# Weight loads of a two-layer mixer and mixture-of-experts kernel: halves, earlier slots, gathers among products

## The chip, the cores and the metric

One core of one Trainium2 chip. The metric is the device time of one launch in microseconds (us); lower is better. Times inside an execution are counted from the start of its span.

## The reference

Two layers on 256 tokens of width 1024, all float32. Layer 0 has a mixer of mLSTM and RG-LRU, layer 1 one of S5 and gated linear attention (GLA). Each is followed by a layer norm over `ALPHA * h + mixer(h)`, then a mixture of experts, then a second norm:

```python
scores = sigmoid(x @ router_w)            # 64 experts, 8 groups
... 8 experts per token, from the 4 best groups
h = silu(x @ w_gate[e]) * (x @ w_up[e])   # [tokens of e, 256]
y = (h @ w_down[e]) * weight              # summed over the 8 experts
out = y + (silu(x @ sw_gate) * (x @ sw_up)) @ sw_down
```

The gate, up and down weights of an expert are 1 MB each, so the experts of a layer are 64 x 3 MB.

## The kernel before

The stages run one after another: `mix0`, `moe0`, `mix1`, `moe1`. Each engine has its program written out by hand, with semaphores between them; SP issues nearly all transfers, in program order, on one DMA queue.

**Where weights go.** The dense weights (mixer, shared expert) pass through `weight_ring`, two halves of 2 MB: `ring_load` (L273) waits until the reader of the load two before is done (`ring_free`, L260), then issues. The experts' weights go to four slots of `expert_weights`, three parts each: gate, up, down (`expert_load` L305, `first_load` L375). The mixers use the same memory for their own data, so slots can be filled only when that data is dead.

**The experts on PE.** `pe_moe` starts with the shared expert's gate and up products (`shared_up`, L995 to L1039, products at L999), for which it waits for the ring half `sh_gu`; the router's products and DVE's choice of experts run between. Then experts go in pairs, 32 a layer. Pairs with even numbers use slots 0 and 1, odd ones slots 2 and 3. For each pair `octets` (L1103) does:
- the gate and up products over eight chunks `c` (L1124, two experts side by side), after waits for the weights, and then counts `gu_full`;
- the scatter of the pair before (L1050), a turn of the gates, the turn of the hidden values (L1138), and two gathers of token rows for the octet after (`gather`, L1075 to L1082); in the last pairs products of the shared expert's down weights and `ALPHA * h` instead (L1086, L1067);
- the down products (L1168), in two halves of 512 columns, each with its own count (`y_lo_full`, `y_hi_full`).

Before the first pair all eight gathers of the first octet are done (L1180 to L1185), each into one of three banks, and ACT (even `c`) and DVE (odd `c`) copy them out.

**The refills.** In `sp_moe` (L383) the first fill of the slots comes in this order: router weights and bias, ring half `sh_gu`, slots 0 and 1 (layer 0, after the stores of `mix0`) or 0 to 2 (layer 1, after PE's product `o1`), ring half `sh_d`, and after `h_ready` the other slots and the norm's parameters. `group` (L404) then refills: for a pair of slots it waits for `gu_full` of the pair that used them, issues two gates and two ups, waits for `y_hi_full`, issues two downs.

**The mixers where the change touches them.** `sp_mix0` and `sp_mix1` load the ring, store and fetch two S5 tables (`s5_b`, `s5_c`) that `mix0`'s DVE program computes for `mix1`: `dve_s5_inputs` (L1696, twelve operations in two halves) stands before the tiles `cols`, `bc0`, `bc1`, whose banks PE uses next. In `mix1` PE starts with products from the fetched `s5_c` (`pe_direct`, L659, products at L667) as soon as DVE has written a first part of the norm (L1472).

Of the kernel before, what the change touches and what calls it, by code (L numbers as in the profile page):

```python
# [86 lines left out]
def build(nc, A, out, stages=("mix0", "moe0", "mix1", "moe1")):  # L87
    ctx = ExitStack()
    with ctx:
# [112 lines left out]
        for l in range(2):  # L202
            MO[l]["gu_in"] = [sem(f"moe{l}_gu_in{s}") for s in range(NSLOT)]
            MO[l]["d_in"] = [sem(f"moe{l}_d_in{s}") for s in range(NSLOT)]
# [100 lines left out]
        def expert_load(sp, m, l, e, s):  # L305
            src_g = A["exp_w_gate"][l, e].rearrange("(p c) f -> p (c f)", c=KC)
            src_u = A["exp_w_up"][l, e].rearrange("(p c) f -> p (c f)", c=KC)
            sp.dma_start(ew[:, s, 0:EW], src_g).then_inc(m["gu_in"][s], 16)  # L308
            sp.dma_start(ew[:, s, EW:2 * EW], src_u).then_inc(m["gu_in"][s], 16)  # L309
# [47 lines left out]
        def sp_mix1(sp, npass):  # L357
# [13 lines left out]
            for name in ("qk1", "v1", "r1", "glu1", "out_a1", "out_b1"):  # L371
                ring_load(sp, ring_no[name])
            sp_ln_params(sp, k, A["ln1_w"][1], A["ln1_b"][1])

        def first_load(sp, m, l, s):  # L375
            expert_load(sp, m, l, s, s)
            sp.dma_start(ew[:, s, 2 * EW:3 * EW], down_src(l, s)).then_inc(m["d_in"][s], 16)

        EARLY_SLOTS = (2, 3)
# [3 lines left out]
        def sp_moe(sp, l):  # L383
# [5 lines left out]
            ring_load(sp, ring_no[f"sh_gu{l}"])  # L389
            early = EARLY_SLOTS[l] if k else 0  # L390
            if l == 0:
                sp.wait_ge(M1["stored"], 32)
            else:
                sp.wait_ge(*B1.full("o1"))
            for s in range(early):
                first_load(sp, m, l, s)
            ring_load(sp, ring_no[f"sh_d{l}"])
            if k:
                sp.wait_ge(S["h_ready"], TT * k)
            for s in range(early, NSLOT):  # L400
                first_load(sp, m, l, s)
            sp_ln_params(sp, k, A["ln2_w"][l], A["ln2_b"][l])

            def group(base, it):  # L404

                for u in range(2):

                    sp.wait_ge(m["gu_full"], (base - 1) * 2 + u + 1)
                    for s in (2 * u, 2 * u + 1):
                        expert_load(sp, m, l, it * NSLOT + s, s)  # L410
                    sp.wait_ge(m["y_hi_full"], (base - 1) * 2 + u + 1)
                    for s in (2 * u, 2 * u + 1):
                        sp.dma_start(ew[:, s, 2 * EW:3 * EW], down_src(l, it * NSLOT + s)).then_inc(m["d_in"][s], 16)

            with sp.Fori(1, NE // NSLOT) as it:
                group(it, it)
            sp.wait_ge(m["npass"], 1)
            npass = sp.value_load(npass_i[0:1, 0:1], min_val=1, max_val=MAX_PASS)
            with sp.If(npass > 1):
                with sp.Fori(1, npass) as ps:  # L420
                    with sp.Fori(0, NE // NSLOT) as it:
                        group(ps * (NE // NSLOT) + it, it)
# [679 lines left out]

# [1014 lines left out]
```

## Time and profile before

| | |
|---|---|
| median of 3 runs | 1257.88 us (1257.76 to 1260.94) |
| the profiled execution | 1257.82 us |
| its span | 1256.1 us |
| PE busy | 1166.2 us (93%) |
| DVE, ACT, POOL busy | 489.3, 193.3, 47.3 us |
| read from HBM | 456.51 MB, 368 GB/s over the span |
| granted clock of TensorE, mean | 0.995 |

The span is what the profiler saw; the time of an execution is 1.7 us more. PE is TensorE's matmul, SPq the queue of SyncE that issues transfers. A row of the timeline has start, duration, engine, line and operation, and in brackets the idle time before it and what ended it. L numbers are lines of the kernel. A product in float32 is shown as two records.

### The profile page before, as it was taken

Reading aid. Unit: us, or ns where it says so; the run is one execution under the profiler, and the core shown is the slowest. Engines: PE = TensorE matmul, PEld = TensorE weight load, DVE = VectorE, ACT = ScalarE, POOL = GpSimd, SP = SyncE. Lnnn points to the kernel's source line nnn. Section 1 sums busy time; section 2 is a strip of 40 time slices with the busy share of each in tenths; the row PEclk is TensorE's granted clock in tenths of the full one; section 3 lists DMA queues with packets and bytes.
Section 4 is the critical chain, followed back from the end, with each engine's and each line's share of the span. In section 5 each row is a group of like instructions: output and inputs, shape, how many; then the busy total and the mean of one; then the engine's idle time right before and its main releaser. Section 6 shows DMA issues by size and latency. Waiting matters only on the chain.

```text
span 1256.1 us, 17816 instructions
## 1 busy us (share of the span) xinstructions
PE 1166.2 (93%) x7245; PEld 567.4 (45%) x7245; DVE 489.3 (39%) x1059; ACT 193.3 (15%) x330; POOL 47.3 (4%) x78
## 2 busy tenths in 40 slices
PE   9999999988888888999899999999888988889996
PEld 8774833333333333333387657333333333333332
DVE  5994733332323233332327256332333233232224
ACT  3231311111111111110122312111111111111102
POOL 6200100000000000000000001000000000000000
PEclk9999999999999999999999999999999999999999
DMA  9775989999999999999953278999999999999993
GB/s 347 205 301 193 421 344 422 420 421 421 421 421 422 422 422 422 422 421 421 399 176 134 96 288 340 419 420 422 420 421 422 420 422 422 422 422 421 421 422 154
DMA packets 76125, 463.78 MB, mean 369 GB/s; under 512 B 8544, under 2 KB 9888, under 8 KB 25376
## 3 DMA queue, kind: packets, MB, share of 16 engines
q1 hardware_dynamic: 75920, 462.37, 90.5%
q8 instruction: 47, 0.77, 0.2%
q10 hardware_dynamic: 144, 0.52, 0.1%
q14 instruction: 14, 0.11, 0.0%
HBM read 456.51 MB, written 6.36 MB: 368 GB/s over the span
## 4 chain that ended last, share of the span: by engine, by line
PE 51%; DMA 42%; SPq 3%; DVE 2%; issue 1%; ACT 1%; DVEq 0%; POOL 0%; POOLq 0%
DMA expert_weights<-in_exp_w_up 40%; PE bank L1124 23%; PE bank L1168 5%; PE bank L652 4%; PE bank L638 3%; PE bank L999 2%; PE bank L726 2%; PE bank L742 2%; SPq L308 2%; PE bank L1050 1%; PE bank L753 1%; DMA expert_weights<-s_rows 1%; PE bank L1079 1%; SPq L309 1%; DMA s_rows<-hidden 1%
## 5 line engine op out<-in xcount | busy, mean ns | idle before, releaser
L1124 PE MATMUL bank<-expert_weights,weight_ring 128*64 128x512 f32 x1024 | 226.8, 595 | 30.9 <-DMA expert_weights<-in_exp_w_up 30.9
L1168 PE MATMUL bank<-expert_weights,hiddenT 128*32 128x512 f32 x2048 | 233.0, 595 | 10.0 <-ACT weight_ring L1379 5.0
L1989 DVE TENSOR_TENSOR hidden<-silu_gate,bank 128x256 f32<-128x256 f32 x64 | 27.0, 422 | 424.3 <-ACT silu_gate L1388 424.3
L1124 PEld LDWEIGHTS bank<-expert_weights,weight_ring 128*64 128x64 f32 x1024 | 81.1, 137 | 175.5 <-issue 175.2
L1124 PE MATMUL bank<-expert_weights,hT 128*64 128x512 f32 x512 | 118.4, 603 | 30.7 <-DMA expert_weights<-in_exp_w_up 30.4
L1168 PEld LDWEIGHTS bank<-expert_weights,hiddenT 128*32 128x32 f32 x2048 | 60.0, 109 | 146.0 <-issue 119.4
L1124 PE MATMUL bank<-expert_weights,octet_high 128*64 128x512 f32 x512 | 116.0, 592 | 0.0
L1388 ACT ACTIVATE silu_gate<-bank 128x256 f32<-128x256 f32 x64 | 24.6, 385 | 471.1 <-PE bank L1124 471.1
L2001 DVE TENSOR_SCALAR y_top<-bank,slot_gate 128x512 fp32r<-128x512 f32 x64 | 48.1, 751 | 108.1 <-PE bank L1168 108.1
L1124 PEld LDWEIGHTS bank<-expert_weights,hT 128*64 128x64 f32 x512 | 39.5, 138 | 110.1 <-issue 110.1
L1392 ACT ACTIVATE y_top<-bank,slot_gate 128x512 fp32r<-128x512 f32 x64 | 44.0, 687 | 268.7 <-PE bank L1168 268.7
L1124 PEld LDWEIGHTS bank<-expert_weights,octet_high 128*64 128x64 f32 x512 | 42.6, 137 | 67.2 <-issue 67.2
L2008 DVE SCALAR_TENSOR_TENSOR y_low<-bank,slot_gate,y_top 128x512 fp32r<-128x512 f32 x64 | 48.0, 751 | 57.6 <-ACT y_top L1392 57.6
L1079 PE MATMUL bank<-onehot_r,h_top 128*128 128x256 f32 x256 | 67.8, 300 | 0.0
L638 PE MATMUL bank<-hT,weight_ring 128*128 128x256 f32 x304 | 66.6, 380 | 0.0
L1079 PE MATMUL bank<-onehot_r,h_low 128*128 128x256 f32 x256 | 62.7, 279 | 0.0
L638 PEld LDWEIGHTS bank<-hT,weight_ring 128*128 128x128 f32 x304 | 57.4, 190 | 7.8
L1050 PE MATMUL bank<-y_top,onehotT_r 64*128 64x512 f32 x256 | 57.5, 445 | 0.0
L652 PE MATMUL bank<-weight_ring,hT 128*128 128x512 f32 x128 | 56.2, 594 | 0.1
L1050 PE MATMUL bank<-y_low,onehotT_r 64*128 64x512 f32 x256 | 50.5, 390 | 0.0
L2004 DVE SCALAR_TENSOR_TENSOR y_low<-bank,slot_gate,y_top 128x512 fp32r<-128x512 f32 x64 | 48.1, 751 | 2.3
L1079 PEld LDWEIGHTS bank<-onehot_r,h_top 128*128 128x128 f32 x256 | 48.8, 191 | 0.0
(384 smaller groups left out, 1061.5 us busy)
## 6 DMA issues: line engine op xcount, KB each, us to landing
expert_weights<-in_exp_w_gate SPq DMA_DIRECT2D x128, 1024.0 KB, 15.0
expert_weights<-in_exp_w_up SPq DMA_DIRECT2D x128, 1024.0 KB, 17.1
expert_weights<-in_exp_w_down SPq DMA_DIRECT2D x128, 1024.0 KB, 18.7
weight_ring<-in_w_in_even SPq DMA_DIRECT2D x5, 2048.0 KB, 9.9
weight_ring<-in_w_out SPq DMA_DIRECT2D x4, 2048.0 KB, 7.8
weight_ring<-in_w_in_odd SPq DMA_DIRECT2D x4, 2048.0 KB, 10.5
s_c<-expert_weights SPq DMA_DIRECT2D x1, 3072.0 KB, 9.7
expert_weights<-s_c SPq DMA_DIRECT2D x1, 3072.0 KB, 10.3
```

What stands on the lines that cost most here:

```text
L308: sp.dma_start(ew[:, s, 0:EW], src_g).then_inc(m["gu_in"][s], 16)
L638: last = nc.tensor.matmul(B.tile(f"{name}{i}")[:, a * SEQ:(a + 1) * SEQ], w[:, c, (2 * i + a) * P:(2 * i + a + 1) * P], hT[:, c, :], start ...
L652: last = nc.tensor.matmul(B.tile(f"{name}{t}")[:, :], hT[:, c, t * P:(t + 1) * P], w[:, c, :], start=(c == 0), stop=(c == KC - 1))
L1050: nc.tensor.matmul(bank[2 * t + n][:, :], onehotT[slot_rows(t), par, :], part[slot_rows(t), n * 512:(n + 1) * 512], start=False, stop=Fals ...
L1079: last = nc.tensor.matmul(bank[b][:, t * SEQ:(t + 1) * SEQ], part[:, t, c, :], onehot[:, t, :, :].rearrange("p e s -> p (e s)"), start=(pa ...
L1124: last_mm = nc.tensor.matmul(bank[6][a * 2 * CAP:(a + 1) * 2 * CAP, :].rearrange("p (w f) -> p w f", w=2), octet_tokens(l, v, c)[:, 2 * q ...
L1168: last_mm = nc.tensor.matmul(bank[b][by_tile:by_tile + CAP, :], hm[:, j, own:own + CAP], ew_d(2 * u + a)[:, j, half * 512:(half + 1) * 512 ...
L1392: nc.scalar.activation(y_top[:, 512:1024], bank[5][:, :], ACT.Copy, scale=slot_gate[:, u:u + 1])\
L1989: nc.vector.tensor_tensor(hslot[:, :], sg[:, :], bank[6][:, DE:2 * DE], ALU.mult)\
L2001: nc.vector.tensor_scalar(y_top[:, 0:512], bank[4][:, :], slot_gate[:, u:u + 1], None, ALU.mult)\
L2004: nc.vector.scalar_tensor_tensor(out=y_low[:, 0:512], in0=bank[4][:, :], scalar=slot_gate[:, u:u + 1], in1=y_top[:, 0:512], op0=ALU.mult, ...
L2008: nc.vector.scalar_tensor_tensor(out=y_low[:, 512:1024], in0=bank[5][:, :], scalar=slot_gate[:, u:u + 1], in1=y_top[:, 512:1024], op0=ALU. ...
```

## The change

- Gate and up weights come by halves (chunks 0 to 3, then 4 to 7) at the refill of slots 0 and 1 for pair 2 and at the refills for pairs 28 to 31. PE waits for the second half in the middle of its products. The first half for pair 2 is released by a new count, `gu_half`, in the middle of pair 0. The down weights of pair 31 come by halves of their columns.
- Three gathers stand before the first pair; the other five follow one by one behind the products of chunks 0 to 4.
- Layer 0: slots 0 and 1 are loaded ahead of the ring half `sh_gu`. Layer 1: slot 1 is loaded after `y1`, slot 2 after the output weights, slot 0 after `o1`, all before the norm's parameters.
- `dve_s5_inputs` is split: one half stays, the other follows the tiles `bc0`, `bc1`.
- The semaphores of the slots are one per pair of slots; refills of passes after the first follow the same order.

```diff
@@ sp_mix1
-            for name in ("qk1", "v1", "r1", "glu1", "out_a1", "out_b1"):
+            for name in ("qk1", "v1", "r1", "glu1"):
                 ring_load(sp, ring_no[name])
+            sp.wait_ge(*B1.full("y1"))
+            first_load(sp, MO[1], 1, 1)
+            for name in ("out_a1", "out_b1"):
+                ring_load(sp, ring_no[name])
+            first_load(sp, MO[1], 1, 2)
+            sp.wait_ge(*B1.full("o1"))
+            first_load(sp, MO[1], 1, 0)
             sp_ln_params(sp, k, A["ln1_w"][1], A["ln1_b"][1])
@@ sp_moe
-            ring_load(sp, ring_no[f"sh_gu{l}"])
-            early = EARLY_SLOTS[l] if k else 0
             if l == 0:
                 sp.wait_ge(M1["stored"], 32)
-            else:
-                sp.wait_ge(*B1.full("o1"))
-            for s in range(early):
-                first_load(sp, m, l, s)
-            ring_load(sp, ring_no[f"sh_d{l}"])
-            if k:
-                sp.wait_ge(S["h_ready"], TT * k)
-            for s in range(early, NSLOT):
+                for s in (0, 1):
+                    first_load(sp, m, l, s)
+            for name in (f"sh_gu{l}", f"sh_d{l}"):
+                ring_load(sp, ring_no[name])
+            sp.wait_ge(S["h_ready"], TT * k)
+            for s in LATE_SLOTS[l]:
                 first_load(sp, m, l, s)
...
+            def first_refill(ps):
+
+                sp.wait_ge(m["gu_half"], ps + 1)
+                for s in range(2):
+                    expert_half(sp, l, NSLOT + s, s, 0, m["gu_in"][0])
+                sp.wait_ge(m["gu_full"], ps * PAIRS + 1)
+                for s in range(2):
+                    expert_half(sp, l, NSLOT + s, s, 1, m["gu_rest"][0])
+                sp.wait_ge(m["y_hi_full"], ps * PAIRS + 1)
+                for s in range(2):
+                    sp.dma_start(ew[:, s, 2 * EW:3 * EW], down_src(l, NSLOT + s)).then_inc(m["d_in"][0], 16)
+
+            def late_refill(ps, pair):
+
+                u = pair % 2
+                first = 2 * pair - 2 * u
+                sp.wait_ge(m["gu_full"], ps * PAIRS + pair - 1)
+                for part, landed in ((0, m["gu_in"]), (1, m["gu_rest"])):
+                    for s in (2 * u, 2 * u + 1):
+                        expert_half(sp, l, first + s, s, part, landed[u])
+                sp.wait_ge(m["y_hi_full"], ps * PAIRS + pair - 1)
...
+            def refills(ps):
+
+                first_refill(ps)
+                refill(ps * (NE // NSLOT) + 1, 1, 1)
+                with sp.Fori(2, NE // NSLOT - 2) as it:
+                    for u in range(2):
+                        refill(ps * (NE // NSLOT) + it, it, u)
+                for pair in range(PAIRS - 4, PAIRS):
+                    late_refill(ps, pair)
@@ pe_moe, octets
                         for c in range(KC):
                             if opening:
                                 pe.wait_ge(m["xg_hi" if c % 2 else "xg_lo"], n + c // 2 + 1)
+                            if c == KC // 2 and first and v == 0 and q == 2:
+                                pe.wait_ge(m["gu_rest"][0], 192 * ps + 64)
+                            if c == KC // 2 and ending:
+                                pe.wait_ge(m["gu_rest"][u], (128 if u else 192) * ps + 64 * (q // 2 + 2 - u))
...
+                            if opening and c == KC // 2 - 1:
+                                last_mm.then_inc(m["gu_half"], 1)
+                            if opening and c + 3 < KC:
+                                open_gather(ps, c + 3)
...
+                            if ending and q == 3 and half:
+                                pe.wait_ge(m["d_rest"], 32 * ps + 32)
@@ pe_moe, before the pairs
-                for c in range(KC):
-                    if c == 2:
-                        pe.wait_ge(m["sh_hidden"], 1)
-                    if c >= 3:
-                        pe.wait_ge(m["xg_lo" if c % 2 else "xg_hi"], ps * PAIRS + (c - 3) // 2 + 1)
-                    gather(c, opening_banks[c % 3])
+                for c in range(3):
+                    open_gather(ps, c)
@@ dve_mix0
             last.then_inc(M0["xc"], 1)
-            dve_s5_inputs(dve, chain)
+            dve_s5_inputs(dve, chain, 0)
...
                 if hd % 2 == 1:
                     last.then_inc(B.done["d"], 1)
+            dve_s5_inputs(dve, chain, 1)
             dve.wait_ge(*B.read("r1"))
```

`expert_half` and `down_half` are transfers of 512 KB: half of each partition's gate or up row (4 KB), or half of the columns of the two down chunks (2 KB each).

## Rows read from the trace of the kernel before

**Rows 1.** The page, chain that ended last, shares of the span by line.
```profile
DMA expert_weights<-in_exp_w_up 40%; PE bank L1124 23%; PE bank L1168 5%; PE bank L652 4%; PE bank L638 3%; PE bank L999 2%; PE bank L726 2%; PE bank L742 2%; SPq L308 2%; PE bank L1050 1%; PE bank L753 1%; DMA expert_weights<-s_rows 1%; PE bank L1079 1%; SPq L309 1%; DMA s_rows<-hidden 1%
```

**Rows 2.** Stretches: busy by engine, then granted clock, DMA share, GB/s.
```profile
220.00:300.00 80.00, 73.22 (x463) 29.60 (x457) 25.41 (x51) 8.98 (x16) 0.00 (x0) 1.00 1.01 421
```

**Rows 3.** Timeline of SP's queue: start, duration, transfer issued.
```profile
104.75 0.51 SPq L386 DMA_DIRECT2D router_w<-in_router_w  x1
118.28 0.43 SPq L277 DMA_DIRECT2D weight_ring<-in_sh_w_up  x1
121.48 0.49 SPq L377 DMA_DIRECT2D expert_weights<-in_exp_w_down  x1
163.60 0.35 SPq L308 DMA_DIRECT2D expert_weights<-in_exp_w_gate  x1
177.02 0.33 SPq L308 DMA_DIRECT2D expert_weights<-in_exp_w_gate  x1
618.55 0.35 SPq L362 DMA_DIRECT2D expert_weights<-s_c  x1
719.67 0.43 SPq L318 DMA_DIRECT2D ln_b<-in_ln_b  x1
```

**Rows 4.** The same seven transfers, in that order: size, us from issue to landing.
```profile
router_w<-in_router_w SPq DMA_DIRECT2D x1, 256.0 KB, 9.6
weight_ring<-in_sh_w_up SPq DMA_DIRECT2D x1, 1024.0 KB, 7.0
expert_weights<-in_exp_w_down SPq DMA_DIRECT2D x1, 1024.0 KB, 19.1
expert_weights<-in_exp_w_gate SPq DMA_DIRECT2D x1, 1024.0 KB, 4.9
expert_weights<-in_exp_w_gate SPq DMA_DIRECT2D x1, 1024.0 KB, 7.0
expert_weights<-s_c SPq DMA_DIRECT2D x1, 3072.0 KB, 10.3
ln_b<-in_ln_b SPq DMA_DIRECT2D x1, 512.0 KB, 10.0
```

**Rows 5.** Chain that ended last in order of time: start, us, what.
```profile
132.50 4.70 PE bank L999 x40
...
152.52 3.87 PE bank L1079 x32
156.39 7.02 PE bank L1124 x32
...
751.78 4.70 PE bank L999 x40
```

**Rows 6.** PE's timeline, pairs 28 and 31 of each layer, first half of the products.
```profile
566.56 3.65 PE L1124 MATMUL bank<-expert_weights,hT 128*64 128x512 f32 x16 [0.82 <-DMA expert_weights<-in_exp_w_up]
...
611.44 3.65 PE L1124 MATMUL bank<-expert_weights,hT 128*64 128x512 f32 x16 [1.02 <-DMA expert_weights<-in_exp_w_up]
...
1186.77 3.65 PE L1124 MATMUL bank<-expert_weights,hT 128*64 128x512 f32 x16 [1.16 <-DMA expert_weights<-in_exp_w_up]
...
1231.31 3.65 PE L1124 MATMUL bank<-expert_weights,hT 128*64 128x512 f32 x16 [0.89 <-DMA expert_weights<-in_exp_w_up]
```

**Rows 7.** PE's timeline at its two longest waits for expert weights.
```profile
357.52 3.65 PE L1124 MATMUL bank<-expert_weights,hT 128*64 128x512 f32 x16 [2.59 <-DMA expert_weights<-in_exp_w_up]
...
977.43 5.15 PE L1124 MATMUL bank<-expert_weights,hT 128*64 128x512 f32 x16 [2.51 <-DMA expert_weights<-in_exp_w_up]
```

**Rows 8.** A stretch behind the second of them, columns as in rows 2.
```profile
977.50:978.50 1.00, 1.00 (x4) 0.41 (x6) 0.00 (x0) 0.00 (x0) 0.00 (x0) 0.50 0.98 410
```

**Rows 9.** DVE's timeline at layer 1's norm before the experts.
```profile
745.76 1.42 DVE L1472 SCALAR_TENSOR_TENSOR resid<-resid,ln_mean_var,ln_w 128x512 f32<-128x512 f32 x2
```

**Rows 10.** PE's timeline in `mix0`: the products of v and of o.
```profile
56.18 14.24 PE L652 MATMUL bank<-weight_ring,hT 128*128 128x512 f32 x32
...
89.38 13.90 PE L652 MATMUL bank<-weight_ring,hT 128*128 128x512 f32 x32
```

**Rows 11.** PE's timeline at the start of `mix1`.
```profile
629.61 2.15 PE L667 MATMUL bank<-expert_weights,gathered_xT 128*32 128x96 f32 x48 [2.60 <-DVE resid L1472]
```

More of the change, by code:

```diff
@@ L202, in build @@
         for l in range(2):
[L203 to L204 removed]
+            for name in ("gu_in", "d_in", "gu_rest"):
+                MO[l][name] = [sem(f"moe{l}_{name}{u}") for u in range(2)]
+            MO[l]["d_rest"] = sem(f"moe{l}_d_rest")
+            MO[l]["gu_half"] = sem(f"moe{l}_gu_half")
         ring_in = [sem(f"ring_in{i}") for i in range(2)]
@@ L415, in sp_moe, with refill @@
-            with sp.Fori(1, NE // NSLOT) as it:
-                group(it, it)
+            def refill(base, it, u):
+                sp.wait_ge(m["gu_full"], (base - 1) * 2 + u + 1)
+                for s in (2 * u, 2 * u + 1):
+                    expert_load(sp, m, l, it * NSLOT + s, s)
+                sp.wait_ge(m["y_hi_full"], (base - 1) * 2 + u + 1)
+                for s in (2 * u, 2 * u + 1):
+                    sp.dma_start(ew[:, s, 2 * EW:3 * EW], down_src(l, it * NSLOT + s)).then_inc(m["d_in"][u], 16)
@@ new lines, in late_refill @@
+            def late_refill(ps, pair):
[3 more added lines that the diff above has]
+                for part, landed in ((0, m["gu_in"]), (1, m["gu_rest"])):
+                    for s in (2 * u, 2 * u + 1):
+                        expert_half(sp, l, first + s, s, part, landed[u])
+                sp.wait_ge(m["y_hi_full"], ps * PAIRS + pair - 1)
+                for s in (2 * u, 2 * u + 1):
+                    if pair < PAIRS - 1:
+                        sp.dma_start(ew[:, s, 2 * EW:3 * EW], down_src(l, first + s)).then_inc(m["d_in"][u], 16)
+                    else:
+                        down_half(sp, l, first + s, s, 0, m["d_in"][u])
+                if pair == PAIRS - 1:
+                    for s in (2 * u, 2 * u + 1):
+                        down_half(sp, l, first + s, s, 1, m["d_rest"])
@@ L420, in sp_moe @@
                 with sp.Fori(1, npass) as ps:
-                    with sp.Fori(0, NE // NSLOT) as it:
-                        group(ps * (NE // NSLOT) + it, it)
+                    for u in range(2):
+                        refill(ps * (NE // NSLOT), 0, u)
+                    refills(ps)
             return npass
@@ L1694, in dve_s5_powers, with dve_s5_inputs @@
               .then_inc(M1["powers"], 1)
-        def dve_s5_inputs(dve, chain):
+        def dve_s5_inputs(dve, chain, half):
             mul = lambda out, x, y: nc.vector.tensor_tensor(out, x, y, ALU.mult)
```

56 lines of the change are left out of this document (32 added, 24 removed).

## The prediction

> **What bounds the kernel now.** I read the page first: its chain of waits puts 40% of the span on the landing of the experts' up weights [rows 1]. So the question is where the stream of expert weights binds. The stretches of DMA share answer it. From 220 to 300 us the DMA engines are at a share of 1.01 and 421 GB/s [rows 2], which is all they do anywhere. The stream runs without a gap from the first refill of a layer to its end. In such a stage bytes set the time: making transfers wait less gains nothing; only starting the unbroken stream earlier, or needing less PE work after its last bytes, does. The loads of slots 0 to 3 before the first refill are no part of it: the queue is idle before the refill at 163.60 (that transfer lands 4.9 us after its issue, that is alone [rows 3, 4]).
>
> **Part 1, first refill by halves, gathers among the products.** Before, eight gathers take 3.87 us and the sixteen products of pair 0 take 7.02 us after them [rows 5]; the refill of slots 0 and 1 is issued behind both, at 163.60. Now it is half released after six gathers and half the products: two gathers (0.97) and half the products (3.51) sooner, 4.5 us. But the next gate stays where it was: slots 2 and 3 are refilled when pair 1's products are done, at 177.02, and PE does no less work up to there. That transfer lands after 7.0 us, against 4.9 us for one that finds the queue empty [rows 3, 4]: the queue had 2.1 us of backlog. A stream started 4.5 us sooner uses up these 2.1 us and then stands idle for the rest. So the start gains 2.1 us at most. Changing between gathers and products five times more, with a DVE queue that does the last eviction later, I bound at 0 and 0.5 us and take 0.2: no row has that change ten times over, and the eight gathers have little wait of their own to lose. Start: -1.9 us. I use layer 0's rows for layer 1 as well: -1.9 us there.
>
> **Part 2, last four pairs by halves.** PE is idle 0.82 us before pair 28 and 1.02 us before pair 31 in layer 0, 1.16 and 0.89 us in layer 1, each time for the up weights [rows 6]; before pairs 29 and 30 it hardly waits, since their share of the shared expert fills the time. With the first halves some 5 us sooner these waits go: -1.9 us in layer 0, about -2.05 us in layer 1. Not more: PE is then busy without a break from pair 27 on, and 3.5 us (half a pair's products) would be had only where PE had been waiting. The down weights by halves gain nothing on top.
>
> The price of the halves: four transfers of 512 KB where there were two of 1 MB, per expert pair twice that. In a full queue six 1 MB transfers land over (121.48+19.1)-(118.28+7.0) = 15.3 us [rows 3, 4], 2.55 us each, so what a transfer alone takes beyond that (4.9 us) is overlapped. Bounds: 0 (all overlapped) and 0.45 us per added transfer (an issue slot of SP's queue [rows 3]); nearest is the overlapped case, and I take 0.4 us in all per layer, late. PE has 1.7 us to spare for the last second half: pair 31 starts at 611.44-1.9 and wants it 3.5 us later, at 613.0, and it lands at 611.3. So in layer 1 the 0.4 us is hidden. The Trainium skill (DMA: Bandwidth & Descriptors, section Bandwidth) speaks against it: it wants 1 MiB per DMA for 75% of the peak. By its fit of 2.0 us plus bytes, if nothing overlapped, each split would cost 2 us, an estimate of some 36 us per layer; the 2.55 us spacing of 1 MB transfers says that most of that is hidden here.
>
> **Part 3, slots loaded earlier, layer 0.** This is where I expect a loss. SP used to issue the shared gate and up weights (up at 118.28) and slots 0 and 1 behind them. Now the slots go first, right behind the router weights that are issued at 104.75 and land at 114.35 [rows 3, 4]; they cannot go sooner, since SP waits for a free half of the ring in front of those. The queue takes transfers in order: slots 0 and 1 until 114.35+15.3 = 129.65, then the shared gate and up, 2 x 2.55, at 134.75. PE asks for them at 132.50 [rows 5], when it begins the shared expert. So PE stands still for 2.3 us plus the semaphore, 2.4 us, where it did not wait before. Bounds: 0 (the queue gets through the parameters faster than their landings show) and 3.3 us (if the bias row behind the router weights costs its own microsecond). All routing and the opening of the experts are behind that wait on PE, in order, so it passes on in full.
>
> It also endangers the clock. An idle time of 2.51 us on PE before 977.43 is followed by sixteen products in 5.15 us, the same sixteen after 2.59 us at 357.52 take 3.65 [rows 7]: behind the one the granted clock is 0.50 [rows 8], the lower level (1.2 GHz), behind the other it is full. Waits up to 1.16 us show nothing of that [rows 6]. I take a fall, 1.5 us; its bounds are 0 and 3.
>
> The slots themselves gain nothing: nobody waits for them in the trace of before.
>
> **Layer 1's slots.** Slot 1 goes into an idle queue. Slots 2 and 0 stand before the norm's parameters, which were issued at 719.67 and landed at 729.7; they now land 15.3 us later, at 745.0. DVE uses them at 745.76 [rows 9]. The shared gate and up land after router weights and 5.1 us more, about 750.9, and PE wants them at 751.78 [rows 5]. The output weights behind SP's new waits are bound to products that PE does later than those waited for. Cost 0, margins below 1 us; cover gone, it costs what they are late.
>
> **Part 4, the S5 inputs in two parts on DVE.** DVE's instructions are the same. The tile products of v take 14.24 us where the same thirty-two take 13.90 for o [rows 10]: 0.34 us for a bank that DVE frees late. -0.3 us. The store of the S5 rows is 3 us later and nobody waits for it.
>
> **What is late next in layer 0.** The mixer of layer 1 starts with PE at 629.61, for DVE's result [rows 11]. It also needs the stored S5 outputs, and they land at 618.55+10.3 = 628.85 [rows 3, 4], 0.76 us before PE starts, or 0.66 us with the semaphore's 0.1. They are last in the queue, so they move with the stream, not with PE's tail. Stream of layer 0: -0.3 +2.4 +1.5 -1.9 +0.4 = +2.1. They land at 630.95, PE starts at 631.05: layer 0 ends +1.4 us. Part 2's 1.9 us in layer 0 are lost in this wait, and would be mostly lost without the clock's fall too.
>
> **Sum.** +1.4 in layer 0, -1.9-2.05 = -3.95 in layer 1: -2.5 us. The profiled execution took 1257.82 us (span 1256.1 and 1.7 around it), the median of the runs is 1257.88, so either start gives the same: 1255.3 us. A measurement of this kernel can tell 0.3% from no change, that is 3.8 us; the forecast is inside it.
>
> **Rivals.**
> A. The clock does not fall (357.52 speaks for it, 977.43 against). Layer 0: the S5 outputs land at 629.45, PE at 629.6: 0. Total -3.95: 1253.9 us.
> B. The shared weights come in time (the queue is further along than the landings say). Stream of layer 0 -1.8, PE starts at 627.15, -2.5. Total -6.4: 1251.4 us.
> C. The other side: a price per transfer on the DMA queue that overlap does not hide. Place: the sixteen added transfers of pairs 28 to 31 and two more at the down weights, of each layer. With c us each, layer 0's stored outputs are 18c late instead of the 0.4 in the sum, layer 1's last second half is 16c late with 1.7 us free. Change = 1.0+18c + (-3.95 + max(0, 16c-1.7)); zero at c = 0.14 us. At SP's issue time of 0.45 us it is 1.0+8.1-3.95+5.5 = +10.6: 1268.5 us. For it: halves this small are nowhere back to back in the trace. Against it: 2.55 us per MB fits the steady 421 GB/s with nothing left per transfer. This is the skill's rule as a mechanism, weaker.
> D. The parameters or shared weights of layer 1 are late as well, by 1 to 2 us, and take back part of layer 1: 1256.3 to 1257.3 us, more with a second fall of the clock.
>
> **Chances.** Forecast 0.38, A 0.25, B 0.17, C 0.12, D 0.08. Below 1254.1 us (faster) lie B, about half of A and the edge of the forecast: 0.33. Slower by over 3.8 us needs C at over 0.25 us per transfer or D with everything against it: 0.09. The rest, 0.58, is no difference. Range: from B, 1251.2, to a small C or D, 1258.4.
>
> **What would show it.** PE idle some 2.4 us before the first shared product at 132 us, with the granted clock at 0.5 behind it or not. The refill of slots 2 and 3 in pair 1 landing 4.9 us after its issue, with a gap of about 2 us in the DMA share before it. No idle time on PE before pairs 28 to 31. PE's idle time before the direct products of layer 1 (629 us) put down to the DMA of the stored S5 outputs instead of DVE. The forecast is wrong if PE does not wait at 132 us (B), if the second halves of pairs 28 to 31 are waited for (C), or if the stream gains more than 2.1 us at the start.

## The result, and the profile after

| | before | after |
|---|---|---|
| median of 5 runs each | 1257.88 us (1257.23 to 1260.94) | 1263.68 us (1262.48 to 1265.2) |
| profiled execution, span | 1257.82, 1256.1 us | 1264.43, 1262.7 us |
| granted clock, mean | 0.995 | 0.991 |

The ratio is 1.0043 [1.0033, 1.0054]: slower by 5.4 us (the medians lie 5.8 us apart), outside the predicted range of 1251.2 to 1258.4 us.

The page of the changed kernel, chain that ended last by line. A transfer of shared weights has entered it with 1% of the span; the up weights of the experts have gone from 40% [rows 1] to 35%:

```profile
DMA expert_weights<-in_exp_w_up 35%; PE bank L1192 24%; PE bank L1241 6%; PE bank L695 5%; PE bank L709 4%; PE bank L1056 3%; PE bank L783 2%; PE bank L1107 2%; DMA weight_ring<-in_sh_w_up 1%; SPq L310 1%; PE bank L1136 1%; PE bank L810 1%; PE bank L799 1%; SPq L311 1%; PE bank L1143 1%
```

**Shared weights of layer 0.** SP's queue of the changed kernel (compare [rows 3]): router weights, bias, the first and the last transfer of slots 0 and 1, the shared up weights behind them:

```profile
104.14 0.58 SPq L409 DMA_DIRECT2D router_w<-in_router_w  x1
104.77 0.44 SPq L411 DMA_DIRECT2D router_bias<-in_router_bias  x1
105.25 0.46 SPq L310 DMA_DIRECT2D expert_weights<-in_exp_w_gate  x1
...
108.64 1.05 SPq L400 DMA_DIRECT2D expert_weights<-in_exp_w_down  x1
...
117.67 0.43 SPq L279 DMA_DIRECT2D weight_ring<-in_sh_w_up  x1
```

Size and us from issue to landing of four of them (router weights, bias, last down weights, shared up):

```profile
router_w<-in_router_w SPq DMA_DIRECT2D x1, 256.0 KB, 9.9
router_bias<-in_router_bias SPq DMA_DIRECT2D x1, 32.0 KB, 11.0
expert_weights<-in_exp_w_down SPq DMA_DIRECT2D x1, 1024.0 KB, 22.9
weight_ring<-in_sh_w_up SPq DMA_DIRECT2D x1, 1024.0 KB, 18.8
```

So the bias lands at 104.77+11.0 = 115.8, the slots are full at 108.64+22.9 = 131.5 (15.7 us for six transfers), and the up weights land at 136.47. PE's timeline shows the wait for them:

```profile
130.00 1.88 PE L799 MATMUL bank<-weight_ring,expert_weights 128*128 128x512 f32 x4
136.52 6.51 PE L1056 MATMUL bank<-hT,weight_ring 128*128 128x128 f32 x40 [4.63 <-DMA weight_ring<-in_sh_w_up]
```

and the stretches after it the granted clock falling to 0.50, its lower level (columns as in [rows 2]):

```profile
136.00:138.00 2.00, 1.48 (x8) 1.49 (x9) 1.48 (x3) 1.54 (x1) 1.51 (x2) 0.73 0.77 209
138.00:140.00 2.00, 2.00 (x11) 2.00 (x11) 0.00 (x0) 1.97 (x3) 2.00 (x2) 0.50 0.86 340
```

The forty products take 6.51 us; in kernel 1 below, where PE doesn't wait for them, PE's timeline has 4.87 (the 4.70 of [rows 5] is counted from the end of the product before). From the first shared product to the gathers the changed kernel loses 5.66-4.18 = 1.5 us by the table below, kernels 2, 3 and 4 with the same wait 2.3, 2.2 and 2.0.

**The opening.** PE's timeline, two rounds of four products of a chunk and one gather of four records:

```profile
159.47 1.08 PE L1192 MATMUL bank<-expert_weights,weight_ring 128*64 128x512 f32 x4
160.47 0.39 PE L1136 MATMUL bank<-onehot_r,h_top 128*128 128x256 f32 x1
160.70 0.28 PE L1136 MATMUL bank<-onehot_r,h_low 128*128 128x256 f32 x1
160.82 0.28 PE L1136 MATMUL bank<-onehot_r,h_top 128*128 128x256 f32 x1
160.93 0.28 PE L1136 MATMUL bank<-onehot_r,h_low 128*128 128x256 f32 x1
161.14 1.08 PE L1192 MATMUL bank<-expert_weights,weight_ring 128*64 128x512 f32 x4
```

A round takes 161.14-159.47 = 1.67 us. By [rows 5] it was 7.02/8 + 3.87/8 = 1.36 us. Five rounds: 1.6 us. The engine has no idle time in between; every step from one kind of product to the other costs a part of it.

**The last pairs and what follows.** PE's timeline at pairs 27, 28 and 31 of layer 0 and at the direct products of `mix1`:

```profile
558.59 5.80 PE L1192 MATMUL bank<-expert_weights,weight_ring 128*64 128x512 f32 x26 [1.99 <-DMA expert_weights<-in_exp_w_up]
...
572.57 3.65 PE L1192 MATMUL bank<-expert_weights,hT 128*64 128x512 f32 x16
...
616.08 3.66 PE L1192 MATMUL bank<-expert_weights,hT 128*64 128x512 f32 x16
...
637.77 2.15 PE L724 MATMUL bank<-expert_weights,gathered_xT 128*32 128x96 f32 x48 [6.14 <-issue]
```

The idle times of [rows 6] are gone. But the direct products, after 2.60 us for DVE before [rows 11], now start after 6.14. The bracket names nothing; SP's queue does. The last four downs keep SP at issuing for 8.49 us; behind them in its program stand the ring load and the fetch of the stored S5 outputs:

```profile
604.76 8.49 SPq L324 DMA_DIRECT2D expert_weights<-in_exp_w_down  x4
614.89 0.56 SPq L279 DMA_DIRECT2D weight_ring<-in_w_in_odd  x1
623.21 0.34 SPq L378 DMA_DIRECT2D expert_weights<-s_c  x1
```

```profile
expert_weights<-s_c SPq DMA_DIRECT2D x1, 3072.0 KB, 14.5
weight_ring<-in_w_in_odd SPq DMA_DIRECT2D x1, 2048.0 KB, 15.2
```

The fetch lands at 623.21+14.5 = 637.7, PE starts at 637.77. Before it was 628.85. The downs do not delay its issue: in both kernels SP issues it 0.1 us behind the products of pair 31 (618.55 behind 618.45, now 623.21 behind 623.10), for which it waits. What is late is the queue in front of it. The ring load now lands at 614.89+15.2 = 630.1, 6.9 us behind the issue of the fetch; before it landed at 598.41+23.0 = 621.4, 2.9 us behind.

PE's timeline at five places in layer 0 and four in layer 1, as the difference to the kernel before in us (the start of an instruction in one profiled execution each; "pair 0 done" is the first scatter behind its gate and up products, "pair 31 done" that behind the last). It serves the kernels below, by their numbers (kernel 10 is left out):

| | L0 shared | gathers | pair 0 done | pair 31 done | direct products | L1 shared | gathers | pair 0 done | pair 31 done |
|---|---|---|---|---|---|---|---|---|---|
| before, at | 132.34 | 152.27 | 163.33 | 618.45 | 629.61 | 751.62 | 772.05 | 783.11 | 1238.33 |
| after | +4.18 | +5.66 | +7.26 | +4.65 | +8.16 | +8.82 | +8.25 | +9.86 | +6.55 |
| 1 shared first | -0.46 | -0.46 | +1.20 | -1.03 | +2.36 | +3.04 | +2.58 | +4.16 | +3.29 |
| 2 plain opening | +4.00 | +6.33 | +6.33 | +2.84 | +6.54 | +7.06 | +6.58 | +6.58 | +3.39 |
| 3 whole late | +4.09 | +6.29 | +7.89 | +6.55 | +6.53 | +6.85 | +6.37 | +7.98 | +7.04 |
| 4 before, slots first | +6.29 | +8.33 | +8.33 | +9.28 | +9.25 | +9.31 | +9.04 | +9.04 | +9.48 |
| 5 shared first, plain | -0.53 | -0.50 | -0.49 | -3.23 | +0.35 | +1.29 | +0.75 | +0.75 | -0.88 |
| 6 late halves only | +0.88 | +0.89 | +0.89 | -0.86 | +2.64 | +3.72 | +3.36 | +3.36 | +1.69 |
| 7 first halves only | -0.48 | -0.47 | -0.45 | -0.31 | -0.33 | +0.21 | +0.06 | +0.06 | +1.22 |
| 8 stored first | -0.53 | -0.52 | -0.52 | -2.56 | -2.58 | +1.29 | +0.75 | +0.76 | -1.76 |
| 9 split columns | -0.48 | -0.48 | -0.48 | +9.73 | +9.71 | +9.87 | +9.60 | +9.60 | +20.29 |
| 11 as 8, whole first refill | -0.59 | -0.57 | -0.57 | -2.84 | -2.85 | -0.84 | -1.39 | -1.39 | -3.89 |
| 12 early slots only | -0.38 | -0.36 | -0.36 | -0.09 | -0.11 | +0.41 | -0.04 | -0.04 | +0.52 |

A column of a single execution is good to about a microsecond (the same parts give 1 us more or less from kernel to kernel), so sizes of whole parts are taken from the timed ratios and places from here. The profiled executions of kernels 1 and 4 took 3.4 and 2.6 us more than the medians of these kernels.

### The profile page after: what moved, and what is told of

Its sections match the earlier page's. It is cut to its first block, busy times and chain, and to the rows that moved or that the text cites. A ratio compares the mean times of both kernels' runs of the same rounds, so it can differ in the third digit from the quotient of the medians.

```text
span 1262.7 us, 17658 instructions
## 1 busy us (share of the span) xinstructions
PE 1170.5 (93%) x7245; PEld 546.8 (43%) x7245; DVE 489.3 (39%) x1059; ACT 193.2 (15%) x330; POOL 47.1 (4%) x78
## 4 chain that ended last, share of the span: by engine, by line
PE 58%; DMA 37%; SPq 2%; issue 1%; DVE 1%; ACT 1%; DVEq 0%; POOL 0%; POOLq 0%
DMA expert_weights<-in_exp_w_up 35%; PE bank L1192 24%; PE bank L1241 6%; PE bank L695 5%; PE bank L709 4%; PE bank L1056 3%; PE bank L783 2%; PE bank L1107 2%; DMA weight_ring<-in_sh_w_up 1%; SPq L310 1%; PE bank L1136 1%; PE bank L810 1%; PE bank L799 1%; SPq L311 1%; PE bank L1143 1%
## 5 line engine op out<-in xcount | busy, mean ns | idle before, releaser
L1192 PE MATMUL bank<-expert_weights,weight_ring 128*64 128x512 f32 x1024 | 230.7, 600 | 30.8 <-DMA expert_weights<-in_exp_w_up 30.8
L1192 PEld LDWEIGHTS bank<-expert_weights,weight_ring 128*64 128x64 f32 x1024 | 70.2, 137 | 182.6 <-issue 128.6
L1192 PEld LDWEIGHTS bank<-expert_weights,hT 128*64 128x64 f32 x512 | 33.9, 136 | 108.4 <-issue 65.7
L1192 PEld LDWEIGHTS bank<-expert_weights,octet_high 128*64 128x64 f32 x512 | 36.7, 137 | 73.2 <-issue 72.0
## 6 DMA issues: line engine op xcount, KB each, us to landing
weight_ring<-in_w_in_odd SPq DMA_DIRECT2D x4, 2048.0 KB, 10.2
```

The costliest lines, as they stand in the source:

```text
L1192: last_mm = nc.tensor.matmul(bank[6][a * 2 * CAP:(a + 1) * 2 * CAP, :].rearrange("p (w f) -> p w f", w=2), octet_tokens(l, v, c)[:, 2 * q ...
```

## The experiments

The kernel before was timed on the same chip beside each group, at medians of 1258.2 to 1258.8 us. A thousandth of the ratio is 1.26 us.

**1. Shared weights ahead of the slots again.**

```diff
+            ring_load(sp, ring_no[f"sh_gu{l}"])
             if l == 0:
                 sp.wait_ge(M1["stored"], 32)
                 ...
-            for name in (f"sh_gu{l}", f"sh_d{l}"):
-                ring_load(sp, ring_no[name])
+            ring_load(sp, ring_no[f"sh_d{l}"])
```

> The changed kernel with one step undone: in layer 0 the shared expert's gate and up weights are issued ahead of slots 0 and 1 again. Theory Q (the order of the queue: these weights land 4 us late and the idle time lets the clock fall): PE no longer waits before the first shared product, no fall of the clock there, gathers of layer 0 begin 5.8 us sooner, and all of it arrives at the end: 1263.7 - 5.8 = 1257.9 us, within 1 us. Theory P (a price per halved transfer is what made the kernel slower, and the wait at 132 us is made up for later by the stream): less than 2 us faster, 1262 us or more.

Measured: 1257.78 us, 0.9998 [0.9988, 1.0007]; against the changed kernel's 1.0043 that is -5.6 us. PE's timeline shows the shared products without an idle time, near their old length:

```profile
131.88 4.87 PE L1056 MATMUL bank<-hT,weight_ring 128*128 128x128 f32 x40
```

As expected to 0.1 us. So the order of these transfers carries the whole loss. What it leaves is a change worth nothing: 5.98 us of idle time stand ahead of the direct products.

**2. All eight gathers ahead of pair 0 again.**

```diff
-                for c in range(3):
+                for c in range(KC):
                     open_gather(ps, c)
...
-                            if opening and c + 3 < KC:
-                                open_gather(ps, c + 3)
```

> The changed kernel with all eight gathers ahead of pair 0 again; the first refill keeps its halves, the first of them released after half of the products. Theory I (each change between gathers and products costs TensorE time, 0.34 us per chunk, five times): the opening takes 1.6 us less in each layer, the gate of the second refill comes 1.6 us sooner in each, total -3.2 us, 1260.5 us. Rival (the opening is hidden, since the stream of weights had 5 us of earlier start to live on): within 1 us of 1263.7.

Measured: 1261.45 us, 1.0031 [1.0017, 1.0045], that is 1.5 us less than with the gathers interleaved (2.2 by the medians; the intervals overlap). The theory has 3.2, its rival at most 1. In both layers the 1.6 us between "gathers" and "pair 0 done" are gone from the table.

**3. The last four pairs whole again.**

```diff
-                with sp.Fori(2, NE // NSLOT - 2) as it:
+                with sp.Fori(2, NE // NSLOT) as it:
...
-                for pair in range(PAIRS - 4, PAIRS):
-                    late_refill(ps, pair)
```

> The changed kernel with pairs 28 to 31 loaded whole, as before the change; first refill, opening and slots stay changed. Theory P' (halves cost the queue some 0.1 us for each added transfer, seen only where the last transfer of the queue is waited for): the stored S5 outputs land 1.9 us sooner relative to the stream, but PE's tail is 2 us longer in both layers; layer 0 gives back about 1.5 us, layer 1 loses 2 us, total +0.5 us, 1264.2. Theory P (halves cost much): 2 us or more faster than 1263.7, since neither layer would pay them.

Measured: 1265.54 us, 1.0056 [1.0039, 1.0073], 1.6 us more than with the halves; the intervals overlap. Where: in layer 0 pair 31 is done 1.9 us later, yet the direct products start 1.6 us sooner. The late halves lengthen what is before the direct products and shorten only layer 1's end. Theory P is out, since the kernel is not faster without them.

**4. Only that order, in the kernel before.**

```diff
-            ring_load(sp, ring_no[f"sh_gu{l}"])
...
             for s in range(early):
                 first_load(sp, m, l, s)
+            if l == 0:
+                ring_load(sp, ring_no[f"sh_gu{l}"])
```

(layer 1 keeps its order)

> The kernel before with one part of the change alone: in layer 0 slots 0 and 1 are issued ahead of the shared gate and up weights. Theory Q: PE idle 4 us or more before the first shared product at 132 us, the granted clock at 0.5 behind it, 1257.9 + 5.8 = 1263.7 us. Theory P: the stream catches up, no more than 1 us slower than before.

Measured: 1264.74 us, 1.0045 [1.0029, 1.0062]: this one exchange costs 5.7 us, as much as undoing it gave back. PE's timeline:

```profile
138.63 7.07 PE L1001 MATMUL bank<-hT,weight_ring 128*128 128x128 f32 x40 [4.66 <-DMA weight_ring<-in_sh_w_up]
```

The wait is the changed kernel's (4.63). PE is 1.6 us later than before already when it begins to wait, and its timeline in `mix0` shows where: in the middle of the products of v it waits for DVE. In kernel 1 it doesn't, though DVE begins its S5 work at the same time. DVE and PE of kernel 4, then of kernel 1:

```profile
50.17 1.23 DVE L1700 TENSOR_TENSOR expert_weights<-expert_weights 128x1024 f32<-128x1024 f32 x1 [2.57 <-DMA expert_weights<-s_rows]
...
64.77 7.13 PE L654 MATMUL bank<-weight_ring,hT 128*128 128x512 f32 x16 [1.67 <-DVE gate_cols L1552]
```

```profile
50.17 1.22 DVE L1768 TENSOR_TENSOR expert_weights<-expert_weights 128x1024 f32<-128x1024 f32 x1 [2.25 <-DMA expert_weights<-s_rows]
...
56.07 13.90 PE L709 MATMUL bank<-weight_ring,hT 128*128 128x512 f32 x32
```

That is the split of DVE's S5 work, which kernel 1 has and kernel 4 has not. The stored S5 rows reach DVE at another time in each profile. Without the split PE loses nothing when DVE begins at 47.54 (kernel 9), 0.34 us at 48.69 (the kernel before), 1.28 at 49.56 (kernel 6) and 1.67 here; with it nothing even at 50.72 (kernel 11). Kernel 4's and kernel 6's marks contain that.

**5. Both undone: shared weights first, plain opening.** Edits 1 and 2 together.

> The changed kernel with two parts undone at once: layer 0's shared gate and up weights ahead of slots 0 and 1 again, and all eight gathers ahead of the first pair. Kept: halves at the first refill, halves for the last four pairs, layer 1's slots early, the split of VectorE's S5 work. If the two undone parts add (order: -5.9 us in the first kernel; interleaving: -2.2 in the second), it takes 1255.5 to 1256.5 us here, 0.998 of the kernel before. If the interleaving only cost time in company of the late shared weights, it comes out with the first kernel, 1257.8. Places: layer 0's first gu_full within 0.3 us of the kernel before, layer 1's at most 3 us behind it, the wait for the stored S5 outputs still there ahead of the direct products (5 to 6 us).

Measured: 1256.88 us, 0.9986 [0.9977, 0.9995]. From kernel 1 that is again 1.5 us (0.9 by the medians, and the intervals overlap here too): as far as can be told, the interleaving costs the same with the shared weights late or in time. The median lies 0.4 us above the expected span. The wait ahead of the direct products is now alone to be seen:

```profile
629.96 2.15 PE L724 MATMUL bank<-expert_weights,gathered_xT 128*32 128x96 f32 x48 [6.20 <-issue]
```

**6. Late halves and nothing else.** The kernel before with the halves for pairs 28 to 31 (kernel 5 with the first refill whole, and layer 1's slots and DVE's S5 work in their old places):

```diff
-                first_refill(ps)
+                refill(ps * (NE // NSLOT) + 1, 1, 0)
                 refill(ps * (NE // NSLOT) + 1, 1, 1)
```

> The kernel before plus halves for the last four pairs of each layer, and nothing else of the change. On record before the first run this was worth -1.5 in layer 1 and nothing in layer 0, less 0.4 of added transfers. Theory now: 18 added transfers cost the queue 2 to 3 us per layer; in layer 0 that delays the landing of the stored S5 outputs, so the direct products begin 1 to 3 us later than before; in layer 1 the last pairs end 1 to 2 us sooner. Sum -1 to +1, 1257.8 to 1259.8 us. Rival: halves cost nothing, the tail gain stands in both layers: 1255 to 1256, direct products no later than before.

Measured: 1258.64 us, 1.0000 [0.9991, 1.0009]. From pair 0 to the end of pair 31 the table has -1.75 us in layer 0 and -1.67 in layer 1: the tail's gain is real in both. In layer 0 the wait takes it back and 1.75 us more (2.64-0.89), since the stored outputs are issued at 617.70 and land 14.5 us later, behind the ring load. The second half of pair 31 is itself waited for, 0.47 us in layer 0 (0.76 us in layer 1 of kernel 5), a sign that the prediction gave for rival C. The DMA queue is full in that stretch and yet moves 413 GB/s, not 421 [rows 2]:

```profile
560.00:600.00 40.00, 40.00 (x233) 14.46 (x231) 11.10 (x22) 3.41 (x6) 0.00 (x0) 1.00 1.02 413
```

**7. First halves and nothing else.** The kernel before with the first refill by halves, all gathers ahead of it (kernel 5 with edit 3, and layer 1's slots and DVE's work as before).

> The kernel before plus halves at the first refill of each layer, and nothing else of the change. The prediction took 2.1 us per layer for the shorter backlog, 1255 here. Theory now, from stretches of the other kernels: 1.2 to 1.4 us per layer, since halves of 1 MB pairs move slowly where they stand alone in the queue (229 to 344 GB/s): pair 27 of layer 0 starts 1.0 to 1.5 us sooner than before and the kernel takes 1256 to 1256.8 us. Rival: no gain at all (the queue loses in slow halves what it gains in an earlier start): 1258.8.

Measured: 1259.14 us, 1.0003 [0.9994, 1.0012]. The time of my theory (1256 to 1256.8) was not met; by the interval a gain is under 0.8 us. SP's queue does start 4 us sooner (the first half's gate, against 163.60 in [rows 3]), and stretches of this kernel show what comes of it:

```profile
159.56 0.33 SPq L318 DMA_DIRECT2D expert_weights<-in_exp_w_gate  x1
```

```profile
160.00:166.00 6.00, 5.80 (x37) 2.86 (x37) 1.68 (x5) 0.97 (x2) 0.00 (x0) 1.00 0.79 214
166.00:168.00 2.00, 2.00 (x24) 0.62 (x20) 0.53 (x2) 0.00 (x0) 0.00 (x0) 1.00 1.02 406
```

The same stretches of the kernel before, which has nothing to do until 164:

```profile
164.00:166.00 2.00, 1.97 (x17) 1.41 (x13) 1.11 (x4) 0.46 (x1) 0.00 (x0) 1.00 0.73 168
166.00:168.00 2.00, 1.82 (x20) 0.63 (x24) 0.69 (x1) 0.13 (x1) 0.00 (x0) 1.00 1.00 422
```

In the first of these six us the queue moves 66 GB/s, in the other five 244, little more than half its rate. Over the whole of 156 to 190 us, by which both streams are full, it moved 361 GB/s against 350:

```profile
156.00:190.00 34.00, 33.59 (x200) 12.60 (x201) 11.02 (x24) 3.52 (x8) 0.00 (x0) 1.00 0.94 361
```

```profile
156.00:190.00 34.00, 33.57 (x202) 12.61 (x200) 11.21 (x25) 3.86 (x7) 0.00 (x0) 1.00 0.86 350
```

That is 11 x 34 = 374 KB or 0.9 us of transfer. The 0.45 us by which this kernel is ahead anyway are not in it: taken 0.45 us sooner, from 155.55 to 189.55, its stretch has 361 GB/s too. The next refill's gate lands 6.9 us after its issue, 7.0 before [rows 4]. In layer 0 the lead reaches PE, as the theory said of pair 27: that pair starts at 550.03, before at 551.64, 1.6 us sooner or 1.2 beyond the 0.45. It is lost again in front of pair 31:

```profile
564.92 3.65 PE L1183 MATMUL bank<-expert_weights,hT 128*64 128x512 f32 x16 [0.80 <-DMA expert_weights<-in_exp_w_up]
...
611.13 3.65 PE L1183 MATMUL bank<-expert_weights,hT 128*64 128x512 f32 x16 [2.40 <-DMA expert_weights<-in_exp_w_up]
```

There PE waits 2.40 us and not 1.02 [rows 6]; in layer 1 no lead forms. One profile can't tell whether that wait belongs to the halves. So 4 us sooner became 0.9 us of queue and nothing in the time.

**8. The stored S5 outputs ahead of the ring load.** Kernel 5 and:

```diff
-            ring_load(sp, ring_no["u1"])
             sp.wait_ge(MO[0]["gu_full"], npass * PAIRS)
             sp.dma_start(ws1[:, 6144:12288], A["s5_c"]).then_inc(M1["c_in"], 16)
+            ring_load(sp, ring_no["u1"])
```

> The kernel of the first of these runs with one exchange in SP's order: the fetch of the stored S5 outputs goes ahead of the load of mixer 1's first weights into the ring. If PE's wait ahead of the direct products (6 us) is the landing of that fetch behind the ring load, the landing comes 3.5 to 4.5 us sooner and the kernel takes 3 to 4 us less than that one: 1251.5 to 1253.5. The ring load then lands 631 to 633 us, first used 4.9 us after the direct products begin, so it is no new wait. Rival: the queue is full either way and what lands last decides; then the gain is under 1 us and a wait of the same size stands ahead of the products that read the ring.

Measured: 1255.97 us, 0.9980 [0.9971, 0.9989], only 0.9 us below kernel 5, and the intervals overlap. PE's timeline:

```profile
627.03 2.12 PE L723 MATMUL bank<-expert_weights,gathered_xT 128*32 128x96 f32 x48 [2.60 <-DVE resid L1538]
...
633.22 3.15 PE L735 MATMUL bank<-hT,weight_ring 128*128 128x128 f32 x16 [1.89 <-DMA weight_ring<-in_w_in_odd]
```

The wait is DVE's again, 2.60 us as in [rows 11], and the products start 2.9 us sooner. But 1.89 us come back where PE wants the ring, and the sixteen products behind that wait take 3.15 us, in kernel 11 behind a wait of 1.09 us 2.05: from 634 to 637 us the granted clock is 0.50 here, and 1.00 there. Kernel 8:

```profile
634.00:637.00 3.00, 3.00 (x16) 3.00 (x15) 0.00 (x0) 0.00 (x0) 0.00 (x0) 0.50 0.91 366
```

The theory was right in that the landing of the stored outputs was the wait. The rival was right on the time and on a new wait at the ring, but not on why: the queue is not full either way. SP issues the fetch only when pair 31's products are done, and the ring load behind it now has to wait for that too. It is issued at 616.38, in kernel 5 at 607.02, and meanwhile the queue runs nearly empty (share 0.24, in kernel 5 1.06):

```profile
614.00:616.00 2.00, 2.00 (x12) 0.54 (x8) 0.00 (x0) 0.00 (x0) 0.00 (x0) 1.00 0.24 93
```

```profile
weight_ring<-in_w_in_odd SPq DMA_DIRECT2D x1, 2048.0 KB, 16.8
```

It lands at 616.38+16.8 = 633.2, just when PE gets it. An order that fills this gap was not tried.

**9. Every refill cut along the columns.** The price of a half by itself: the kernel before with 120 more transfers per layer, waited for as before.

```diff
+            for part in range(2):
+                lo, hi = part * EW // 2, (part + 1) * EW // 2
+                for w, name in ((0, "exp_w_gate"), (1, "exp_w_up")):
+                    ...
+                    sp.dma_start(ew[:, s, w * EW + lo:w * EW + hi], src[:, lo:hi]).then_inc(m["gu_in"][s], 16)
```

> The kernel before with every refill's gate and up load cut in two along the columns (512 KB each, rows of 4 KB in place of 8 KB), all issued at the same place as before and waited for together: 120 transfers more per layer, nothing gained by finer waits. If an added half costs the queue 0.10 to 0.18 us, as the last four pairs showed (1.9 to 3.2 us for 18), this takes 12 to 22 us per layer more: 1282 to 1302 us. If the price of the halves is only that of their number in the tail or of their thin filling of the queue, the time stays within 5 us of the kernel before: 1258 to 1263.

Measured: 1279.05 us, 1.0163 [1.0147, 1.0178]: 20.2 us for 240 halves, 0.084 us each. The expectation, from the last four pairs, had 1282 at least; so halves in the steady stream cost less than it took. By the table the cost grows evenly, 10.2 us in layer 0 (9.73+0.48) and 10.7 in layer 1 (20.29-9.60). The queue's stretch is as full as before, at 413 GB/s:

```profile
220.00:300.00 80.00, 69.52 (x447) 28.46 (x435) 24.80 (x50) 8.98 (x16) 0.00 (x0) 1.00 1.02 413
```

**10. The same number of transfers, cut between partitions 63 and 64.** Rows of 8 KB, as before the change.

```diff
+                    rows = slice(64 * part, 64 * part + 64)
+                    sp.dma_start(ew[rows, s, w * EW:(w + 1) * EW], src[rows, :]).then_inc(m["gu_in"][s], 16)
```

> As the kernel cut along the columns, but cut between partitions 63 and 64: the same 120 more transfers per layer of 512 KB, with rows of 8 KB as before. If a transfer has a price for itself, this one takes as long as the other cut. If it is the shorter rows that move slowly, it takes within 4 us of the kernel before: 1257 to 1262. If 64 partitions fill the queue worse, it is the slower of the two.

Measured: 2078.9 us, four runs of 2025 to 2106. It is the third case named, by far. The same stretch shows the queue full at nearly half the rate:

```profile
220.00:300.00 80.00, 40.81 (x235) 15.80 (x231) 13.84 (x28) 4.97 (x9) 0.00 (x0) 0.75 1.02 230
```

So it says nothing on rows of 4 KB against a price per transfer; this stays open. The Trainium skill (SBUF — State Buffer, section "Door 1: The DMA port swizzle") says that partitions 0 to 63 reach only 8 of the 16 ports, with an asymptote of some 218 GB/s. The 230 GB/s, with transfers to either half in turn, lie 5% above that and fit it.

**11. Kernel 8 with the first refill whole.** The edit is that of kernel 6.

> The kernel with the stored S5 outputs fetched first (1255.97), with the first refill whole again: kept are halves for the last four pairs, layer 1's slots early, the split of VectorE's S5 work and the new place of the fetch. If the halves of the first refill bring nothing, as they did alone (1.0003), it takes 1255.5 to 1256.5 us here. If they bring 1.0 us per layer in company of the late halves, 1257.5 to 1258.

Measured: 1255.80 us, 0.9976 [0.9967, 0.9986], as low as with the halves (1255.97). As expected: the first refill's halves bring nothing in company either. This is the best version found: 3.0 us below the kernel before and 8 below the changed one. In layer 0 the last pairs' gain now reaches the direct products (-2.85 us); by layer 1's shared products -0.84 is left, of which the ring took part:

```profile
632.62 2.05 PE L735 MATMUL bank<-hT,weight_ring 128*128 128x128 f32 x16 [1.09 <-DMA weight_ring<-in_w_in_odd]
```

**12. Layer 1's slots early and DVE's S5 work in two parts, and nothing else.** Kernel 5 with edits 3 and 6.

> Of the change only what the other kernels did not try by itself: layer 1's slots 1, 2 and 0 loaded as mixer 1 is done with each, ahead of its parameters, router weights and shared weights, and the split of VectorE's S5 work; everything else as in the kernel before. If these are worth nothing, since the loads of that time are covered by the mixer and router (layer 1's shared products began within 1 us of the distance they had before in every kernel), it takes 1257.8 to 1258.8 us, ratio 0.999 to 1.000. Rival D of the prediction: layer 1's shared weights or LN parameters land late behind the slots, 1259.5 or more. A gain of 0.3 (the split alone) is too small to be told by the median; it would show as layer 0's first shared product 0.4 to 0.6 us sooner.

Measured: 1257.44 us, 0.9992 [0.9983, 1.0001]: no difference that can be told. The first shared product is 0.38 us sooner; but it is 0.48 sooner in kernels 7 and 9, which have no split, so this difference doesn't measure the split. Its worth, by the profiles named under kernel 4, is 0 to 1.7 us, depending on when the stored rows arrive.

## Why the prediction was wrong

**The account by parts**, from timed ratios: order of layer 0's loads +5.6 and +5.7 us (kernels 1, 4); interleaving +1.5, twice (2, 5); halves at the last pairs 0.0 alone (6), -1.6 in company (3); halves at the first refill +0.4 alone (7), +0.5 in company (11 to 8); the rest -1.0 (12), at the edge of its interval. Alone, with the two +1.5 as one: 5.7+1.5+0.0+0.4-1.0 = 6.6, measured 5.4.

**Shared weights of layer 0: right in place and mechanism, mis-sized.** The step put the slots directly behind the router weights and "took" 2.4 us of wait, with 3.3 as its bound should the bias cost a microsecond of its own. It did: the slots begin at 115.8, not 114.35, take 15.7 and not 15.3 us, and the shared weights land at 136.47, not 134.75. PE was also ready 0.45 us sooner than in the profile before (not by the split alone: kernels 7 and 9 are so too without it), so the wait was 4.63 us, past the bound. The clock fell as forecast and took 1.5 us here (2.0 to 2.3 in kernels 2 to 4) against 1.5, so rivals A and B are out. At the gathers that is +5.66 us instead of -0.3+2.4+1.5 = +3.6.

**Layer 0 as a whole** was put at +1.4 us and is +8.16 at the direct products. It is +5.66 at the gathers, +7.26 behind pair 0 and +4.65 behind pair 31, and the wait for the stored outputs adds 3.5.

**The S5 work in two parts: "-0.3 us".** The reading of [rows 10] was right for that execution and no measure of the part: the loss it removes was 0 to 1.7 us in the profiles without the split (kernels 4, 6, 7, 9).

**Opening interleaved: "I take 0.2", measured 1.6 us per layer on PE.** The failed step says that no row has the change of product kind often. The bounds 0 and 0.5 were set without a row, and it was called nearest to the lower one. In the time of the kernel it is 1.5 us for both layers (2.2 by the medians), less than twice 1.6; that the first half is then released earlier against the end of pair 0 might explain the rest, but was not tried by itself.

**Start of the stream: "the queue had 2.1 us of backlog", so -2.1.** The backlog is there, but the halves don't use it up. The sum assumed that bytes started 4.5 us sooner move at the queue's full rate until it runs dry, while that of kernel 7 in these 6 us is 214 GB/s. The sign it gave, the refill of slots 2 and 3 landing after 4.9 us, did not come: it is 6.9 us in kernel 7 and 6.7 in the changed one. The stream gained 0.9 us in kernel 7's layer 0, and the time 0. Why PE gives that up before pair 31 stays open.

**Tail: -1.9 and -2.05 us, right in size** (-1.75 and -1.67 by kernel 6, with the halves' price in them), and right that layer 0's is lost in the wait for the stored outputs.

**The price of the halves: "I take 0.4 us in all per layer".** The steady price is 0.084 us each (kernel 9), 18 x 0.084 = 1.5 us. In layer 0 of kernel 6 the stored outputs land at 617.70+14.5 = 632.2, against 628.85 before: 3.35 us, less 0.89 by which that kernel was late already, leaves 2.5, 0.14 us for each of the 18 (the ring load in front gives the same: 624.8 against 621.4). The tail's price is thus above the steady one, in one profile. Rival C put the zero of its sum at 0.14 us. Its mechanism acts, but in layer 0's wait alone, and the kernel with it alone is at 1.0000. The argument that 2.55 us per MB leaves nothing per transfer was no evidence: it was taken from whole transfers and could not show what halves need. The Trainium skill's fit of 2.0 us plus bytes (DMA: Bandwidth & Descriptors, section "Anatomy of one DMA — SWDGE (gpsimd) path"), by which the prediction estimated 36 us per layer if nothing overlapped, is more than ten times the 1.5 to 2.5 us measured in a full queue.

**Layer 1** was put at -3.95 and is 6.55-8.16 = -1.6 in the changed kernel's profile, the interleaving's 1.6 and the missing start among it. Rival D did not occur (kernel 12).

## What to carry to other kernels

Before a load is moved ahead of another in a full queue, add up what the displaced one now waits behind, small parameter transfers too, and find who needs it first: here 6 MB that nobody waited for cost 4.6 us of PE and 1.5 to 2.3 us of clock. A steady GB/s of whole transfers doesn't show what halves cost: measure that by splitting all of them. And where a shorter tail is followed by a fetch in the same queue, look at what stands in front of it, or the tail's gain ends in its wait; but what is moved behind the fetch also takes over what the fetch waits for (kernel 8). Don't take the worth of a part from one execution: look at the same wait in several profiles.

## What the runs showed that was not expected

- SP itself is held at issuing when many transfers are under way: the last four downs take 8.49 us of its queue, where two took 0.81 us at 169.88 in the kernel before. In kernel 9 one up takes 5.08 us at 250.60. What is written behind them is issued later: the ring load at 614.89, 598.41 before. How many transfers it takes was not measured.
- Halves of 512 KB move at 214 GB/s in the six us after the first of them (244 without the first us), and at 413 in a full queue, against 421 for whole ones.
- PE's idle time of 1.89 us in kernel 8 is followed by a granted clock of 0.50, that of 1.09 us at the same place in kernel 11 by 1.00.
- Transfers over 64 of the 128 partitions, to both halves in turn, run at 230 GB/s in a queue at a share of 1.02.
- A gather of four records between products takes 0.67 us, in a row of gathers 3.87/8 = 0.48 [rows 5]; the four products take 1.00 instead of 0.88.
